# Two reorderings in a nine-stage fp32 transformer kernel: residual adds ahead of weight splits on VectorE, and table transposes behind the up block on TensorE

## The chip, the cores and the metric

The kernel runs on one core of one Trainium2 chip. The metric is the device time of one execution in microseconds (us), lower is better. PE is the matrix engine (TensorE), PEld its weight loads, ACT is ScalarE, DVE is VectorE, POOL is GpSimd, and SP is the engine that issues most of the DMAs (transfers between the chip's large memory and the on-chip buffer).

## The reference

Two transformer blocks run over 256 tokens of width 2048, all in fp32. What matters here are the three feed-forward networks, since the change lies in them:

```python
D_MODEL = 2048; SEQ = 256; D_FF = 4 * D_MODEL; D_FF_2 = 5632
def sqrelu_mlp(x, w_up, w_down):              # block 1, twice
    h = jax.nn.relu(x @ w_up)
    return (h * h) @ w_down
...
        x = layer_norm(DEEPNORM_ALPHA * x + h, ln_mix_g[i], ln_mix_b[i])
        x = layer_norm(DEEPNORM_ALPHA * x + sqrelu_mlp(x, w_up[i], w_down[i]), ...)
...
def _conv_ffn(h, w_up, conv_w, conv_b, w_down):   # block 2, once
    a = h @ w_up
    a = causal depthwise convolution of width 3 over the tokens (a) + conv_b
    gate, val = jnp.split(a, 2, axis=-1)
    return (jax.nn.silu(gate) * val) @ w_down
...
def _s5_group(...):   # block 2: 64 groups of 16 channels, 64 complex states each
    abar, bbar from lambda, dt, b;  s_t = abar * s_(t-1) + bbar * u_t;  y = Re(c s) + d u
```

Around them stand a pooling mixer, a dilated attention and a mixer of a state-space scan and a low-rank attention. The state-space scan is done four tokens at a step with small matrices ("tables") that follow from lambda, dt, b and c. Building these tables is independent of the tokens.

## The kernel before

All weights stream through four slots of 128 x 2048 values each (`raw`, 1 MB a slot). The matrix engine takes fp32 data as a sum of a high part and a low part, so each slot passes through four hands: SP loads `raw[s]`; ACT copies it rounded to `whi[s]` (`hi1`, L528); DVE subtracts the two to `wlo[s]` (`lo1`, L1028); PE does three matmuls for each product (L1807 to L1809 for up tiles, L1855 to L1857 for down tiles) and counts `chunk_used`. `hi1` of a slot waits until the previous use of the slot is over, and SP's next load of it waits for `lo1` (`lo_ready`). Four slots' worth of weights are a quad. The order on each engine is written out by hand, and semaphores (`then_inc`, `wait_ge`) tie the engines together.

The stages run one after the other: pooling, mlp0, attention, mlp1, the mixer, and ffn. In mlp0 and mlp1 the 8192 hidden features are done in 16 groups of 512. A turn of PE's loop does `up(g + 1)` (192 matmuls of 256 columns into PSUM banks 0 and 1) and `down(g)` (four chunks of 24 matmuls of 512 columns each). Chunk `s` of `down` makes 512 output columns for all tokens in two PSUM banks; it alternates between banks 4, 5 and banks 6, 7. DVE adds each finished chunk to `resid` (`add_down`, L1068) and thereby frees the banks through `down_free`. Chunk 2 may start only when the add of chunk 0 is done, chunk 3 only after that of chunk 1. ACT reads the up block (`activate`, L646 and L648: relu and square) and later rounds it for the next down (`split`). In ffn there are 11 groups, each with two up quads (gate and value), a convolution that ACT and DVE share (L986, L1654), and one down quad.

In mlp0 alone, 16 table jobs run beside the weights, one in each turn. POOL builds the operands `b_wide`, `c_wide` and `b_four` of a job from `compact`; `ssm_tables` on PE turns them and multiplies them (L1926 four transposes, L1931 the products, into banks 2 and 3); ACT's `table_out` copies the result out, stores it by DMA, and loads `compact` for the next job. The lines that close this ring are:

```python
# ACT, table_out(j), called after activate(g + 1)
act.wait_ge(job_turned, j + 1)
...
if not last:
    load_compact(j + 1)
# POOL, job j
pool.wait_ge(compact_landed, j * 16 + 16)
pool.wait_ge(tables_stored, j * 48 + 48)
...
pool.sem_inc(job_ready, 1)
# PE, ssm_tables(j)
pe.wait_ge(job_ready, j + 1)
pe.wait_ge(job_copied, j + 1)
```

Of the kernel before, what the change touches and what calls it, by code (L numbers as in the profile page):

```python
# [156 lines left out]
def build(nc, x_t, x_rows, gain_rows, weights, ssm_compact, ssm_skip, features, consts, dist_table, ssm_lam, positions, out):  # L157
    with ExitStack() as ctx:
# [130 lines left out]
        def wait_used(eng, q, s=SLOTS - 1):  # L289

            eng.wait_ge(chunk_used, q * SLOTS + (SLOTS + s + 1))
# [730 lines left out]
        def _(dve):  # L1022
            step = Steps(dve, dve_steps)

            def lo1(q, s, width=CW):

                dve.wait_ge(hi_ready, q * SLOTS + (s + 1))
                dve.tensor_tensor(wlo[:, s, 0:width], raw[:, s, 0:width], whi[:, s, 0:width].bitcast(F32),  # L1028
                                  ALU.subtract).then_inc(lo_ready, 1)
# [5 lines left out]
            def lo4_add(q, q_down, widths=(CW,) * 4):  # L1035

                for s in range(SLOTS):
                    lo1(q, s, widths[s])
                    add_down(q_down, s)

            def norm(name, gain, src, dst_hi, dst_lo, fill=False):
                k = NORM[name]
# [22 lines left out]
            def add_rows(nb, bank, sem_, n):  # L1065

                r = rows_of(resid, nb)
                return dve.tensor_tensor(r, r, ps[:, bank:bank + 2, :], ALU.add).then_inc(sem_, n)  # L1068
# [110 lines left out]
            def add_down(q, nb):  # L1179
                wait_used(dve, q, nb)  # L1180
                add_rows(nb, 4 + 2 * (nb % 2), down_free, 2)
# [200 lines left out]
            q, u = QUAD["pool_out"], UNITS["pool_out"]  # L1382
# [67 lines left out]
            q, u = QUAD["attn_out"], UNITS["attn_out"]  # L1450
# [26 lines left out]
            q, base = QUAD["mixer"], UNITS["mlp1"] + 120  # L1477
# [169 lines left out]
            def conv_rest(g, half_):  # L1647

                dve.wait_ge(conv_start, g * 2 + (half_ + 1))
                for lag, tap in ((1, 1), (2, 0)):  # L1650
                    for nt in range(4):
                        i = g * 4 + (half_ * (FF2 // P) + nt)
                        o = conv[:, 4 * half_ + nt, lag:T]
                        ins = dve.scalar_tensor_tensor(out=o, in0=block_ps(half_)[:, nt, 0:T - lag],  # L1654
                                                       scalar=fcol("ffn_conv_w_2", i + tap * (2 * FF2 // P)), in1=o,
                                                       op0=ALU.mult, op1=ALU.add)
                        if lag == 1:
                            step(ins)
                    if lag == 1:
                        step.settle()  # L1660
                ins.then_inc(conv_done, 1)
                dve.wait_ge(conv_done, g * 2 + (half_ + 1))
                dve.sem_inc(block_free, 1)

            def group(g, q, adds):

                conv_rest(g, 0)
                lo1(q, 0)
                dve.wait_ge(sig_ready, g + 1)
                if not (isinstance(g, int) and g == 0):  # L1670
                    dve.wait_ge(hidden_lo, g + h0)
                step(dve.tensor_tensor(hid[:], conv[:, 0:4, :], gate_sig[:], ALU.mult))
                for s in range(1, SLOTS):
                    lo1(q, s)
                conv_rest(g, 1)
                for s in range(SLOTS):
                    lo1(q + 1, s)
                    if adds:
                        add_down(q, s)
                    if s == 0:  # L1680
                        step.settle()
                        dve.tensor_tensor(hid[:], hid[:], conv[:, 4:8, :], ALU.mult).then_inc(hidden_ready, 1)
                dve.wait_ge(hidden_hi, g + (h0 + 1))
                dve.tensor_tensor(hid_lo[:], hid[:], hid_hi[:].bitcast(F32), ALU.subtract).then_inc(hidden_lo, 1)
# [15 lines left out]
            q, base = q0 + 3 * n - 1, UNITS["ffn"] + 8 * (n - 1)  # L1700
# [96 lines left out]
        def _(pe):  # L1797
# [137 lines left out]
            def mlp(name, tables=False):  # L1935
                q0, b0, h0, n = QUAD[name], BLOCK[name], HIDDEN[name], FF // HID

                def up(g):
                    quad_block(g * 2 + (q0 - 1), 0, g + (b0 + 2))
                block_first("mix" + name[-1], q0, b0 + 2)  # L1940
                if tables:
                    pe.wait_ge(table_landed, 48)
                with pe.Fori(0, n - 1) as g:
                    if tables:
                        ssm_tables(g)
                    up(g + 1)
                    down(g * 2 + (q0 + 2), g * 8 + UNITS[name], g + (h0 + 1))
                if tables:
                    ssm_tables(n - 1)
                down_last(q0 + 2 * n - 1, UNITS[name] + 8 * (n - 1), h0 + n, last_hi, last_lo)  # L1950
                if tables:
                    pe.wait_ge(job_copied, JOBS + 1)
                    pe.wait_ge(lags_copied, JOBS + 1)
# [13 lines left out]
            q, u = QUAD["pool_out"], UNITS["pool_out"]  # L1967
# [109 lines left out]
            q, u = QUAD["attn_out"], UNITS["attn_out"]  # L2077
# [355 lines left out]
```

## Time and profile before

| | |
|---|---|
| three runs | 3532.62 us median (3529.07 to 3534.78) |
| profiled execution, its own time | 3528.66 us |
| its span in the profile | 3526.8 us |
| PE busy | 3314.5 us, 94% of the span |
| DVE busy | 1950.6 us, 55% |
| ACT busy | 1461.2 us, 41% |
| POOL busy | 304.4 us, 9% |
| mean busy share of the DMA engines | about half, 174 GB/s |

The span runs from the first to the last instruction of the profiled execution; its own time is 1.9 us longer. PE's busy share is close to full, but the ends of matmuls are modelled, so PE shows as busy for a fraction of a microsecond after its last matmul has streamed. What counts as lost is therefore read from the starts of its instructions and from the waits. The clock that was granted to PE over the whole span is 0.976 of full speed.

### The profile page before, as it was taken

The numbers are of one execution on the slowest core, as the hardware profiler recorded it, in microseconds if no ns is written. First come the engines' busy times: TensorE is split into PE (matmuls) and PEld (weight loads), VectorE is DVE, ScalarE is ACT, GpSimd is POOL, SyncE is SP. The second block draws the span as 40 slices with busy tenths as digits, with TensorE's granted clock in tenths as the row PEclk, the third lists the DMA queues.
The fourth block names the chain that finished last, engine by engine and source line by source line (L and its number), as shares of the span: only waits on it lengthen the run. The fifth ranks groups of instructions, "written<-read, shape, count | busy, mean of one in ns | idle before, by whom it ended". The sixth has DMA issues, their size and how long they took to land.

```text
span 3526.8 us, 54501 instructions
## 1 busy us (share of the span) xinstructions
PE 3314.5 (94%) x22368; PEld 3029.7 (86%) x22368; DVE 1950.6 (55%) x1709; ACT 1461.2 (41%) x1281; POOL 304.4 (9%) x474
## 2 busy tenths in 40 slices
PE   6899999999999999989999999989789999999998
PEld 6778888788878999978988888869677899999897
DVE  7755444444455444546555555577445666655656
ACT  4334343434344434334443434434553444444442
POOL 1301312321330000000000000005000000000000
PEclk9999999999999999999999999999899999999999
DMA  6445555555554444445555555525223555555552
GB/s 255 146 165 202 184 186 177 184 184 186 178 183 156 180 168 158 168 156 203 189 186 184 190 182 187 189 96 219 107 94 132 191 183 186 186 183 189 180 190 95
DMA packets 117687, 613.40 MB, mean 174 GB/s; under 512 B 14480, under 2 KB 45264, under 8 KB 47184
## 3 DMA queue, kind: packets, MB, share of 16 engines
q1 hardware_dynamic: 94640, 594.79, 47.5%
q10 hardware_dynamic: 22944, 17.10, 1.5%
q8 instruction: 82, 1.34, 0.1%
q14 instruction: 21, 0.17, 0.0%
HBM read 599.26 MB, written 12.58 MB: 173 GB/s over the span
## 4 chain that ended last, share of the span: by engine, by line
PE 75%; DVE 6%; POOL 5%; ACT 4%; issue 4%; DMA 3%; ACTq 1%; POOLq 0%; SPq 0%; DVEq 0%
PE ps L1807 17%; PE ps L1809 16%; PE ps L1808 16%; PE ps L1855 7%; PE ps L1856 7%; PE ps L1857 7%; DMA compact<-ssm_compact 2%; POOL b_wide L1770 1%; DMA raw<-weights 1%; POOL b_four L1773 1%; POOL job_tmp L1766 1%; DVE wlo L1028 1%; POOL c_wide L1770 1%; ACT whi L528 1%; DVE conv L1654 1%
## 5 line engine op out<-in xcount | busy, mean ns | idle before, releaser
L1028 DVE TENSOR_TENSOR wlo<-raw,whi 128x2048 fp32r<-128x2048 f32 (+2 forms) x572 | 1254.7, 2199 | 1388.3 <-ACT whi L528 1382.3
L528 ACT ACTIVATE whi<-raw 128x2048 fp32r<-128x2048 f32 (+2 forms) x572 | 1044.0, 1830 | 1690.5 <-PE ps L1809 1007.4
L1807 PE MATMUL ps<-x_pair,whi 128*128 128x256 f32 x5104 | 1438.0, 282 | 56.4 <-DVE wlo L1028 34.2
L1809 PE MATMUL ps<-x_pair,wlo 128*128 128x256 f32 x5104 | 1430.8, 280 | 0.0
L1808 PE MATMUL ps<-x_pair,whi 128*128 128x256 f32 x5104 | 1430.7, 280 | 0.0
L1807 PEld LDWEIGHTS ps<-x_pair,whi 128*128 128x128 f32 x5104 | 963.2, 189 | 61.7 <-issue 52.1
L1808 PEld LDWEIGHTS ps<-x_pair,whi 128*128 128x128 f32 x5104 | 963.0, 189 | 1.3
L1809 PEld LDWEIGHTS ps<-x_pair,wlo 128*128 128x128 f32 x5104 | 963.4, 189 | 0.0
L1855 PE MATMUL ps<-whi,hid_hi 128*128 128x512 f32 x1312 | 529.7, 404 | 37.4 <-DVE resid L1068 30.6
L1857 PE MATMUL ps<-whi,hid_lo 128*128 128x512 f32 x1312 | 524.5, 400 | 0.0
L1856 PE MATMUL ps<-wlo,hid_hi 128*128 128x512 f32 x1312 | 524.3, 400 | 0.0
L1855 PEld LDWEIGHTS ps<-whi,hid_hi 128*128 128x128 f32 x1312 | 250.1, 191 | 112.9 <-DVE resid L1068 48.9
L1857 PEld LDWEIGHTS ps<-whi,hid_lo 128*128 128x128 f32 x1312 | 250.1, 191 | 61.6
L1856 PEld LDWEIGHTS ps<-wlo,hid_hi 128*128 128x128 f32 x1312 | 250.6, 191 | 57.0
L1068 DVE TENSOR_TENSOR resid<-resid,ps 128x1024 f32<-128x1024 f32 x171 | 207.4, 1213 | 0.0
L385 POOL TENSOR_TENSOR scan_room<-state,hop 128x64 f32<-128x64 f32 (+3 forms) x20 | 10.0, 500 | 1363.0 <-ACT state L862 1361.6
L1654 DVE SCALAR_TENSOR_TENSOR conv<-ps,feat,conv 128x255 f32<-128x255 f32 (+1 forms) x176 | 72.6, 475 | 2.7
L1781 POOL TENSOR_TENSOR inner_out<-inner_out,lag_out 128x256 f32<-128x256 f32 x16 | 11.8, 737 | 575.5 <-ACT lag_out L622 575.5
L1770 POOL TENSOR_TENSOR b_wide<-job_tmp 64x128 f32<-64x128 f32 x64 | 54.5, 852 | 4.9
L1773 POOL TENSOR_TENSOR b_four<-job_tmp 64x128 f32<-64x128 f32 x64 | 50.7, 792 | 0.0
L1855 PE MATMUL ps<-whi,x_pair 128*128 128x512 f32 x128 | 50.6, 396 | 0.0
L1856 PE MATMUL ps<-wlo,x_pair 128*128 128x512 f32 x128 | 50.6, 396 | 0.0
(341 smaller groups left out, 2421.9 us busy)
## 6 DMA issues: line engine op xcount, KB each, us to landing
raw<-weights SPq DMA_DIRECT2D x539, 1024.0 KB, 4.8
read_tab<-read_tables SPq DMA_DIRECT2D x2, 3072.0 KB, 12.4
raw<-weights SPq DMA_DIRECT2D x8, 640.0 KB, 8.0
drive_tables<-drive_out ACTq DMA_DIRECT2D x16, 256.0 KB, 6.0
read_tables<-c_wide ACTq DMA_DIRECT2D x32, 128.0 KB, 5.9
drive_tab<-drive_tables SPq DMA_DIRECT2D x4, 1024.0 KB, 6.8
x_in<-x_t SPq DMA_DIRECT2D x4, 512.0 KB, 6.9
resid<-x_rows ACTq DMA_DIRECT2D x1, 2048.0 KB, 14.0
```

The costliest lines, as they stand in the source:

```text
L528: act.activation(whi[:, s, 0:width], raw[:, s, 0:width], ACT.Copy).then_inc(hi_ready, 1)
L1028: dve.tensor_tensor(wlo[:, s, 0:width], raw[:, s, 0:width], whi[:, s, 0:width].bitcast(F32), ALU.subtract).then_inc(lo_ready, 1)
L1068: return dve.tensor_tensor(r, r, ps[:, bank:bank + 2, :], ALU.add).then_inc(sem_, n)
L1654: ins = dve.scalar_tensor_tensor(out=o, in0=block_ps(half_)[:, nt, 0:T - lag], scalar=fcol("ffn_conv_w_2", i + tap * (2 * FF2 // P)), in1= ...
L1770: step(pool.tensor_tensor(wide[rows, e, :, :, 16 * g:16 * g + 16], a[rows], b[rows], ALU.add))
L1773: step(pool.tensor_tensor(b_four[rows, e, :, :, 16 * g:16 * g + 16], a[rows, :, STEP - 1:STEP, :].to_broadcast(same), b[rows, :, STEP - 1: ...
L1807: pe.matmul(o, w_hi, x_hi, start=first, stop=False)
L1808: pe.matmul(o, w_hi, x_lo, start=False, stop=False)
L1809: return pe.matmul(o, w_lo, x_hi, start=False, stop=last)
L1855: pe.matmul(o, xh[:, k, t], whi[:, s, c], start=first and j == 0, stop=False)
L1856: pe.matmul(o, xh[:, k, t], wlo[:, s, c], start=False, stop=False)
L1857: ins = pe.matmul(o, xl[:, k, t], whi[:, s, c], start=False, stop=last and j == 3)
```

## The change

Two orders are changed; no instruction of arithmetic is added or taken away.

On DVE, in the loops of mlp0, mlp1 and ffn, the residual add of slot `s` now stands in front of the weight split of the same slot. On PE, in mlp0's loop, the job's transposes and products now stand behind the up block instead of in front of it. The job of the last turn, behind the loop, stays where it was.

```diff
             def lo4_add(q, q_down, widths=(CW,) * 4):
                 for s in range(SLOTS):
+                    add_down(q_down, s)
                     lo1(q, s, widths[s])
-                    add_down(q_down, s)
...
                 conv_rest(g, 1)
                 for s in range(SLOTS):
-                    lo1(q + 1, s)
                     if adds:
                         add_down(q, s)
+                    lo1(q + 1, s)
                     if s == 0:
                         step.settle()
                         dve.tensor_tensor(hid[:], hid[:], conv[:, 4:8, :], ALU.mult).then_inc(hidden_ready, 1)
...
                 with pe.Fori(0, n - 1) as g:
+                    up(g + 1)
                     if tables:
                         ssm_tables(g)
-                    up(g + 1)
                     down(g * 2 + (q0 + 2), g * 8 + UNITS[name], g + (h0 + 1))
                 if tables:
                     ssm_tables(n - 1)
```

In the program of DVE, in the loop of mlp0, the rows from the fourth split of the down quad on read as follows before. L1028 is a split (`lo1`), L1068 a residual add.

```order
205 L1028 TENSOR_TENSOR wlo<-raw,whi 128x2048
206 L1027 ISA
207 L1028 TENSOR_TENSOR wlo<-raw,whi 128x2048
208 L291 REGISTER_ALU
209 L1068 TENSOR_TENSOR resid<-resid,ps 128x2x512
210 L1027 REGISTER_ALU
211 L1028 TENSOR_TENSOR wlo<-raw,whi 128x2048
212 L291 REGISTER_ALU
213 L1068 TENSOR_TENSOR resid<-resid,ps 128x2x512
```

The same place in the changed kernel:

```order
205 L1028 TENSOR_TENSOR wlo<-raw,whi 128x2048
206 L291 REGISTER_ALU
207 L1068 TENSOR_TENSOR resid<-resid,ps 128x2x512
208 L1027 ISA
209 L1028 TENSOR_TENSOR wlo<-raw,whi 128x2048
210 L291 REGISTER_ALU
211 L1068 TENSOR_TENSOR resid<-resid,ps 128x2x512
212 L1027 REGISTER_ALU
213 L1028 TENSOR_TENSOR wlo<-raw,whi 128x2048
```

Each add has moved ahead of one split; the split of a slot and the add that waits for the same chunk have changed places, four times a turn.

In the program of PE, at the head of mlp0's loop (L1943 is the loop's entry, L1926 and L1931 are the table job, L1807 to L1809 the up block), before:

```order
1538 L1943 UNCONDITIONAL_BRANCH
1539 L1943 ISA
1540 L1926 MATMUL ps<-const,b_wide 128x128 x4
1541 L1931 MATMUL ps<-c_wide,b_four 128x128 x4
1542 L1834 REGISTER_ALU
1543 L1804 ISA
1544 L1807 MATMUL ps<-x_pair,whi 128x256
```

and in the changed kernel, at the end of the up block and the start of the down block (L1855 to L1857):

```order
1735 L1809 MATMUL ps<-x_pair,wlo 128x256
1736 L1926 MATMUL ps<-const,b_wide 128x128 x4
1737 L1931 MATMUL ps<-c_wide,b_four 128x128 x4
1738 L1804 ISA
1739 L1900 ISA
1740 L1855 MATMUL ps<-whi,hid_hi 128x512
1741 L1856 MATMUL ps<-wlo,hid_hi 128x512
```

The eight instructions of the job have moved behind the 192 matmuls of the up block and now stand directly ahead of the down block.

## Rows read from the trace of the kernel before

**Rows 1.** The page: the span and the number of instructions.

```profile
span 3526.8 us, 54501 instructions
```

**Rows 2.** The page's chain that ended last, shares of the span by engine.

```profile
PE 75%; DVE 6%; POOL 5%; ACT 4%; issue 4%; DMA 3%; ACTq 1%; POOLq 0%; SPq 0%; DVEq 0%
```

**Rows 3.** Busy time in the stretches of the mlp0, mlp1 and ffn loops.

```profile
core 0: us, PE busy (x) PEld busy (x) DVE busy (x) ACT busy (x) POOL busy (x), PEclk, DMA share, GB/s
288.00:1050.00 762.00, 715.77 (x4495) 635.92 (x4495) 373.02 (x200) 302.00 (x245) 206.94 (x315) 0.98 0.54 184
1638.00:2318.00 680.00, 678.80 (x4320) 608.23 (x4320) 369.01 (x199) 275.06 (x168) 0.00 (x0) 1.00 0.52 186
2780.00:3486.00 706.00, 704.57 (x5022) 657.34 (x5021) 439.64 (x373) 301.61 (x235) 0.00 (x0) 1.00 0.52 183
```

**Rows 4.** The relu of ACT, one a turn, in mlp0 and in mlp1.

```profile
L646 ACT ACTIVATE hid<-ps x15: 1003/1027/1032, 314.5 to 1024.6; 128x1024 f32<-128x1024 f32 x15
...
L646 ACT ACTIVATE hid<-ps x15: 1002/1004/1007, 1665.2 to 2297.4; 128x1024 f32<-128x1024 f32 x15
```

**Rows 5.** Waits in mlp0, 288 to 1050 us: total, times, longest.

```profile
PE ps L1855 <- DVE resid L1068: 29.3, 15, 2.3
PEld ps L1926 <- POOLq L1778: 21.7, 15, 2.4
PE ps L1926 <- POOLq L1778: 15.1, 14, 2.0
```

**Rows 6.** Timeline of ACT in one turn of mlp0: start, duration.

```profile
566.11 1.91 ACT L528 ACTIVATE whi<-raw 128x2048 fp32r<-128x2048 f32 x1 [3.74 <-PE ps L1809]
...
573.69 1.92 ACT L528 ACTIVATE whi<-raw 128x2048 fp32r<-128x2048 f32 x1 [1.94 <-issue]
```

**Rows 7.** Timeline of DVE in the same turn.

```profile
575.63 2.29 DVE L1028 TENSOR_TENSOR wlo<-raw,whi 128x2048 fp32r<-128x2048 f32 x1 [5.29 <-ACT whi L528]
577.84 1.21 DVE L1068 TENSOR_TENSOR resid<-resid,ps 128x1024 f32<-128x1024 f32 x1
```

**Rows 8.** Timeline of PE in the same turn.

```profile
576.88 0.40 PE L1857 MATMUL ps<-whi,hid_lo 128*128 128x512 f32 x1
579.11 0.50 PE L1855 MATMUL ps<-whi,hid_hi 128*128 128x512 f32 x1 [1.84 <-DVE resid L1068]
...
591.73 0.40 PE L1857 MATMUL ps<-whi,hid_lo 128*128 128x512 f32 x1
592.69 0.66 PE L1926 MATMUL ps<-const,b_wide 128*128 128x128 f32 x4 [0.56 <-POOLq L1778]
...
593.99 0.36 PE L1807 MATMUL ps<-x_pair,whi 128*128 128x256 f32 x1
```

**Rows 9.** Timeline of POOL in the same turn: first and last instruction of the job.

```profile
578.38 0.41 POOL L1765 TENSOR_TENSOR job_tmp<-compact,z_pow 128x128 f32<-128x128 f32 x1 [5.82 <-DMA compact<-ssm_compact]
...
591.47 1.12 POOL L1770 TENSOR_TENSOR c_wide<-job_tmp 64x160 f32<-64x160 f32 x2
```

**Rows 10.** Two of 13 stretches behind the add wait; columns as in Rows 3.

```profile
580.50:583.50 3.00, 3.00 (x9) 2.36 (x8) 2.48 (x2) 0.00 (x0) 2.76 (x4) 0.51 0.75 270
630.00:634.00 4.00, 3.84 (x17) 3.12 (x18) 3.46 (x3) 0.01 (x1) 3.85 (x4) 1.00 0.91 283
```

**Rows 11.** Waits in mlp1, 1650 to 2290 us, and ffn, 2800 to 3480 us.

```profile
PEld ps L1855 <- DVE resid L1068: 6.6, 28, 0.3
...
PEld ps L1855 <- DVE resid L1068: 5.8, 10, 0.6
```

**Rows 12.** Timeline of PE in ffn, from chunk 1 to chunk 2 of a down quad.

```profile
2998.28 0.40 PE L1857 MATMUL ps<-whi,hid_lo 128*128 128x512 f32 x1
...
2999.18 0.39 PE L1856 MATMUL ps<-wlo,hid_hi 128*128 128x512 f32 x1
```

**Rows 13.** The end of ffn: timelines of DVE and PE.

```profile
3490.76 1.21 DVE L1068 TENSOR_TENSOR resid<-resid,ps 128x1024 f32<-128x1024 f32 x1
...
3493.16 0.80 PE L1855 MATMUL ps<-whi,hid_hi 128*128 128x512 f32 x1 [6.65 <-DVE hid_lo L1684]
```

## The prediction

> **What bounds the kernel now.** I read the view of the stages first, then the chain, the waits of PE in each loop, and last the timelines of one turn. The span is 3526.8 us [rows 1]. The chain that ended last is PE for 75% of it, and POOL stands on it with 5%, or some 176 us [rows 2], although of the three feed-forward loops it works in one alone [rows 3]. So in mlp0 work runs through POOL while PE could have more to do. The stages show where: in mlp1 and ffn PE is busy for 99.8% of the stretch and its granted clock is 1.00, the upper of its two levels, 2.4 GHz; in mlp0 it is busy for 715.77 of 762 us and the clock is 0.98 [rows 3]. The reader is to see that mlp0 and mlp1 do the same matrix work, and that one is slower.
>
> By how much, the relu of ACT tells, which comes once a turn. In mlp0 15 of them start between 314.5 and 1024.6 us, 14 turns of 50.72 us; in mlp1 between 1665.2 and 2297.4 us, 14 turns of 45.16 us [rows 4]. The table job of mlp0 takes PE from 592.69 to 593.99 us, 1.30 us [rows 8]. So 50.72 - 45.16 - 1.30 = 4.26 us of each turn are lost to something else.
>
> Three things make it up. PE waits for a residual add in every turn, 29.3 us over 15 waits, 1.95 us each; and it waits for POOL's job in nearly every turn, 15.1 us over 14, 1.08 us each [rows 5]. The clock is the third: in the 3 us behind the add wait of one turn it is 0.51, so at the lower level of 1.2 GHz, and in another turn it is 1.00 [rows 10]. Of the 13 turns that I looked at in this way, 9 show 0.51 to 0.69. Over the loop 0.98 means 2% of 762 us, 15 us, or 1.0 us a turn [rows 3]. 1.95 + 1.08 + 1.0 = 4.0 us; 0.2 us remain, and the weight loads do wait somewhat longer than the matmuls (21.7 against 15.1 us in the case of POOL [rows 5]).
>
> **Why these waits are there.** The add: chunk 1 of the down block has its last matmul at 576.88 us, and chunk 2 starts at 579.11 us, when the add of chunk 0 is through [rows 8]. That add starts at 577.84 us, since it stands behind the split, which starts at 575.63 us [rows 7], which waits for ACT's rounding at 573.69 us [rows 6]. Chunk 0 had been ready for long: up and down stream the same number of columns, so each takes half of 45.16 us, 22.6 us, and a chunk 5.65 us. The down block started near 566.0 us, as ACT's rounding of the last up slot shows [rows 6], so chunk 0 was done near 571.7 us. ACT's 2 us of rounding, DVE's 2.2 us of splitting and ACT's table work all stand between it and an add that needs none of them.
>
> The job: the ring is up block, relu and copies on ACT, load of `compact`, POOL's 20 operations (578.38 to 592.59 us [rows 9]), transposes, next up block. From the end of the up block to the start of the transposes it takes 592.69 - 566.1 = 26.6 us, and the ring closes with 1.30 us of table work and 22.6 us of up block: 50.5 us, the measured turn. **So mlp0 turns at the pace of this ring, and not of PE's own work.** Taking away the add wait alone would only lengthen the wait for POOL. Both edits are needed together.
>
> **The change, part by part.**
>
> *Transposes behind the up block.* The job of turn g is now wanted a full up block later. The ring no longer runs through POOL within a turn: a job has the whole turn, 46.4 us, for its 26.6, a cover of 19.8 us. On ACT the copy of the tables stands behind a rounding and the two operations of `activate`, 4 us past the end of the up block; the transposes and products now take the first 1.3 us of that time, so the copy isn't late by them. Its five DMA issues, and whatever SP has queued, keep their places: no queue is moved past. The down block starts 1.3 us later and the up block 1.3 us earlier; both sums stay. If the cover were gone, each us of it would cost 1 us a turn.
>
> *Adds ahead of the splits.* The split of a slot waits for ACT's rounding, which waits for the same chunk. The add waits for that chunk alone, so it fits in the 1.9 us in which ACT rounds. In mlp0 the add of chunk 0 ends near 7.1 + 1.3 us after the up block's end, and chunk 2 wants it 12.6 us after. The add wait goes, and with it, I take it, the lower clock, since mlp1, whose turns have no wait of PE of that length, holds 1.00 [rows 3].
>
> New turn of mlp0: 45.16 + 1.30 = 46.46 us, less 0.1 us of add wait that mlp1's own turn still holds (below). 50.72 - 46.4 = 4.3 us. It applies to the 14 turns from the first to the last relu that I counted: 60 us. Ahead of them nothing changes, since the first up block of the loop waits for the relu's banks either way. Behind the last relu little changes: the last job still stands behind the last down block of the loop, its ring of 26.6 us is as long as before, and PE is now at its door after 1.3 + 22.6 = 23.9 us. It waits 2.7 us there instead of 1 to 2, but starts the last table work at the same moment. Unknown is the length of that job: POOL's operations take 0.4 us or, beside a split on DVE, some 2 us more. I bound this at 2 us to either side.
>
> *The same adds in mlp1 and ffn.* In ffn, chunk 1's last matmul starts at 2998.28 us, and the second of chunk 2 at 2999.18 us [rows 12]. Two steps of 5.65 / 24 = 0.235 us would be 0.47; 0.43 us are lost, in each of ten turns: 4.3 us. The bound above is the wait of the weight loads, 5.8 us; below it is 0. In mlp1 the loads wait 6.6 us in 28 waits, two a turn, of 0.24 us [rows 11]. In ffn 0.15 of 0.58 us of each such wait cost the matmuls nothing; the same off 0.24 leaves 0.09 us, 28 times, 2.5 us. I take 2 us, between 0 and 6.6.
>
> *The end.* After the last ffn turn PE waits 6.65 us for `hid_lo`, which stands on DVE behind the add of chunk 3, 1.21 us at 3490.76 us [rows 13]. The add now runs while ACT rounds the last slot, and PE starts 1.2 us sooner. The clock is low there, so it may be 0 to 3 us.
>
> Sum: 60 + 4.3 + 2 + 1.2 = 67.5 us. The profiled execution took 3528.66 us, 1.9 us more than its span, so 3461 us; the median of the three runs is 4 us above that one and would give 3465 us. **I say 3463 us.**
>
> **Rivals.**
>
> *The lower clock stays.* All 15 us of it: 3463 + 15 = 3478 us. For it: in 4 of 13 turns the same wait of 2 us left the clock alone [rows 10], so the wait isn't the whole cause, and two blocks are now separated by small matmuls of the job. Against it: mlp1 has no such time at all. The Trainium skill, "TensorE: Matmul & The Clock Gate", section "A second HAM failure mode: psum-queue depth-cycling", says that frequent short idles between groups of matmuls can make the clock swing between its levels. By that rule, the clock stays low as long as any short idles are left, and the time would be this rival's; in mlp1, with idles of 0.2 us twice a turn, the trace doesn't agree.
>
> *Only one of the two waits goes.* If the ring through POOL still closed a turn (say, because the job's copies on ACT come so late that the cover of 20 us is used up), mlp0 would stay at 50.7 us and only 4.3 + 2 + 1.2 us would be gained: 3521 us against 3528.66, about 3523 on my middle. Against it speak the 19.8 us.
>
> *Slower: the splits come late.* Where ACT's rounding is already there when DVE arrives, the add ahead delays the split by 1.21 us, and with it `lo_ready`, SP's next load of the slot and PE's next use. There are some 160 such adds; if each were on the path, 160 x 1.21 = 194 us would be added, 3463 + 194 = 3657 us at the worst. It decides from the point where a split has less than 1.2 us of slack. The split of slot 0 ends at 577.92 us and PE wants it at 593.99 us, 16 us later [rows 7, 8], some 12 us in the new turn. It would need a third of the splits on the path to end slower than now.
>
> **How the numbers follow.** The forecast has 0.79; the clock that stays 0.11; one wait only 0.07, half of it by more than 0.2%; slower 0.03. This kernel's measurement can tell about 0.2%, 7 us, from no change. So faster is 0.79 + 0.11 + 0.035 = 0.935, same 0.035, slower 0.03. The range: downwards the bounds of mlp1, ffn, the end and the last job give 3461 - 8 = 3453 us; upwards it takes in the clock that stays, 3480 us.
>
> **What would show it.** In the changed profile the relus of mlp0 should stand 46.4 us apart, 14 turns in 650 us, with PE's clock at 0.99 or 1.00 in the loop. No wait of PE for the residual add in mlp0, mlp1 or ffn, and one for POOL instead of 14, of 2 to 4 us, ahead of the last job. PE's wait for `hid_lo` at the end near 5.4 us. POOL's share of the chain should fall from 5% to under 1%. The prediction is wrong if the relus are still 50 us apart (the ring is closed elsewhere), if ACT's table copy waits for the transposes by more than 0.5 us, if `whi` waits for weight loads, which now come at 9% more MB a second, or if the clock in the loop is still 0.98.

## The result: 1.85% faster, as forecast in sum

| | before | after |
|---|---|---|
| median, executions interleaved on one chip | 3530.85 us (4: 3524.75 to 3534.78) | 3464.62 us (4: 3463.76 to 3466.21) |
| profiled execution, its own time | 3528.66 us | 3466.21 us |
| its span | 3526.8 us | 3464.4 us |

The ratio is 0.9815, with a 95% interval of 0.9802 to 0.9827. The forecast was 3463 us, with a range of 3453 to 3480 us.

The page of the changed kernel, its parts 1 (busy time of POOL, last entry) and 4 (the chain that ended last), answers to [rows 1, 2]:

```profile
span 3464.4 us, 54486 instructions
...
PE 3293.8 (95%) x22368; PEld 3029.7 (87%) x22368; DVE 1970.0 (57%) x1709; ACT 1461.4 (42%) x1281; POOL 321.3 (9%) x474
...
PE 89%; DVE 5%; ACT 3%; DMA 2%; issue 1%; POOL 0%; SPq 0%; ACTq 0%; DVEq 0%; POOLq 0%
```

POOL has left the chain, where it held 5%, and PE has gone from 75% to 89%. POOL itself is busy for 321.3 us, 17 us more than before: its work has got slower, and hardly anybody waits for it. That is worth remembering for the first experiment.

The relus of the changed kernel, mlp0 and mlp1, answer to [rows 4]:

```profile
L646 ACT ACTIVATE hid<-ps x15: 1009/1029/1032, 314.5 to 963.6; 128x1024 f32<-128x1024 f32 x15
...
L646 ACT ACTIVATE hid<-ps x15: 1003/1005/1006, 1608.8 to 2239.0; 128x1024 f32<-128x1024 f32 x15
```

A turn of mlp0 takes (963.6 - 314.5) / 14 = 46.36 us instead of 50.72, a turn of mlp1 45.01 instead of 45.16. Over 14 turns that is 61.0 us in mlp0 and 2.0 us in mlp1.

The windows of the changed kernel in the same three loops (columns as in [rows 3]):

```profile
300.00:960.00 660.00, 660.00 (x4297) 599.16 (x4296) 357.52 (x185) 282.57 (x226) 207.80 (x294) 1.00 0.59 199
1581.00:2250.00 669.00, 667.29 (x4280) 602.50 (x4281) 368.52 (x196) 273.26 (x167) 0.00 (x0) 1.00 0.53 187
2730.00:3425.00 695.00, 695.00 (x4964) 650.71 (x4963) 435.51 (x371) 296.97 (x231) 0.00 (x0) 1.00 0.52 184
```

PE is busy through the whole of mlp0's loop, at a clock of 1.00. Its waits from 270 to 1000 us, which answer to [rows 5]:

```profile
PE ps L1926 <- POOLq L1778: 5.4, 1, 5.4
PE ps L1807 <- ACT hid L646: 3.1, 1, 3.1
```

Both kinds of wait of [rows 5] are gone from the turns. One wait for POOL is left, ahead of the last job, and the wait of the first turn for the relu has grown from 1.7 to 3.1 us, since no table job stands ahead of it any more. And at the end of ffn:

```profile
PE ps L1855 <- DVE hid_lo L1684: 5.5, 1, 5.5
```

It was 6.65 us [rows 13].

**Where the gain was given back.** The roundings L998 of ffn start from 2830.7 to 3488.4 us before and from 2774.2 to 3427.8 us after, 657.7 and 653.6 us: 4.1 us. With the 1.1 us at the end the gains come to 61.0 + 2.0 + 4.1 + 1.1 = 68.2 us; the span is shorter by 62.4. Some 4.5 us of the difference lie between the last relu of mlp0 and the first transpose of `resid` on PE (L1870) behind mlp0: 1024.6 to 1073.1 us before, 48.5 us; 963.6 to 1016.6 us after, 53.0 us. They have two parts. From the end of the last up block to the last table job it is 26.7 us before (1022.63 to 1049.30 us) and 29.0 after (961.63 to 990.66 us), so 2.4 us are a job that is ready later. From the table job to L1870 it is 23.8 us before and 25.9 after, 2.1 us for the same work: that is the clock, which is low when PE comes back from a wait of 5.4 us.

The rest, 1.3 us, lies where nothing was changed or is the sum of small differences: from the last relu of mlp1 to the first rounding of ffn it takes 535.2 us instead of 533.3, attention is 0.1 us longer, and from the last rounding of ffn to the end of the span the gain is 1.8 us, 0.7 us more than the shorter wait.

The first turn lost time too, though not in this sum. From the first relu of mlp0 to the second, before and after:

```profile
L646 ACT ACTIVATE hid<-ps x2: 1003/1004/1005, 288.6 to 314.5; 128x1024 f32<-128x1024 f32 x2
L646 ACT ACTIVATE hid<-ps x2: 1005/1007/1009, 287.1 to 314.5; 128x1024 f32<-128x1024 f32 x2
```

It takes 27.4 us instead of 25.9; in the execution that was profiled mlp0 began 1.5 us sooner, which hides it. The windows at both ends show the clock. Before:

```profile
270.00:300.00 30.00, 28.26 (x240) 28.06 (x240) 19.22 (x10) 13.47 (x9) 0.00 (x0) 1.00 0.62 235
...
1020.00:1075.00 55.00, 50.89 (x242) 41.06 (x240) 33.91 (x35) 21.97 (x22) 14.54 (x22) 1.00 0.41 136
```

and after:

```profile
960.00:1015.00 55.00, 49.60 (x223) 40.68 (x223) 30.09 (x30) 21.07 (x22) 16.89 (x22) 0.94 0.38 126
270.00:300.00 30.00, 26.91 (x215) 26.69 (x214) 20.23 (x11) 12.50 (x8) 0.00 (x0) 0.94 0.56 215
```

The clock of 1.00 in the loop has its price at both its ends: 2.1 us behind the last job and 1.5 us in the first turn, after waits that are now longer (5.4 us for the last job, 3.1 us for the relu). 6% of a window would be more than that, because part of the low clock falls into the wait itself, where it costs nothing.

### The profile page after: what moved, and what is told of

Same layout as the page of the kernel before. It is cut to its first block, busy times and chain, and to the rows that moved or that the text cites. A ratio compares the mean times of both kernels' runs of the same rounds, so it can differ in the third digit from the quotient of the medians.

```text
span 3464.4 us, 54486 instructions
## 1 busy us (share of the span) xinstructions
PE 3293.8 (95%) x22368; PEld 3029.7 (87%) x22368; DVE 1970.0 (57%) x1709; ACT 1461.4 (42%) x1281; POOL 321.3 (9%) x474
## 4 chain that ended last, share of the span: by engine, by line
PE 89%; DVE 5%; ACT 3%; DMA 2%; issue 1%; POOL 0%; SPq 0%; ACTq 0%; DVEq 0%; POOLq 0%
PE ps L1807 17%; PE ps L1809 17%; PE ps L1808 17%; PE ps L1855 11%; PE ps L1856 11%; PE ps L1857 11%; DMA raw<-weights 1%; DVE wlo L1028 1%; ACT whi L528 1%; ACT y_mix L874 1%; PE ps L1931 0%; PE ps L2119 0%; PE ps L1846 0%; PE ps L2041 0%; DVE row_stats L1079 0%
## 5 line engine op out<-in xcount | busy, mean ns | idle before, releaser
L1028 DVE TENSOR_TENSOR wlo<-raw,whi 128x2048 fp32r<-128x2048 f32 (+2 forms) x572 | 1259.4, 2207 | 1099.0 <-ACT whi L528 1095.3
L1807 PE MATMUL ps<-x_pair,whi 128*128 128x256 f32 x5104 | 1440.8, 282 | 56.8 <-DVE wlo L1028 32.6
L1809 PE MATMUL ps<-x_pair,wlo 128*128 128x256 f32 x5104 | 1432.9, 281 | 0.0
L1807 PEld LDWEIGHTS ps<-x_pair,whi 128*128 128x128 f32 x5104 | 966.3, 189 | 62.5 <-issue 52.9
L1809 PEld LDWEIGHTS ps<-x_pair,wlo 128*128 128x128 f32 x5104 | 966.9, 189 | 0.0
L1855 PE MATMUL ps<-whi,hid_hi 128*128 128x512 f32 x1312 | 520.0, 396 | 5.5 <-DVE hid_lo L1684 5.5
L1857 PE MATMUL ps<-whi,hid_lo 128*128 128x512 f32 x1312 | 518.5, 395 | 0.0
L1068 DVE TENSOR_TENSOR resid<-resid,ps 128x1024 f32<-128x1024 f32 x171 | 208.7, 1221 | 198.7 <-PE ps L1857 195.7
L1855 PEld LDWEIGHTS ps<-whi,hid_hi 128*128 128x128 f32 x1312 | 246.5, 188 | 64.5 <-DVE hid_lo L1684 6.0
L1857 PEld LDWEIGHTS ps<-whi,hid_lo 128*128 128x128 f32 x1312 | 246.3, 188 | 60.4
L385 POOL TENSOR_TENSOR scan_room<-state,hop 128x64 f32<-128x64 f32 (+3 forms) x20 | 10.1, 503 | 1362.9 <-ACT state L862 1361.5
L1773 POOL TENSOR_TENSOR b_four<-job_tmp 64x128 f32<-64x128 f32 x64 | 59.1, 924 | 0.0
L1770 POOL TENSOR_TENSOR c_wide<-job_tmp 64x160 f32<-64x160 f32 x64 | 51.8, 810 | 4.9
L758 ACT ACTIVATE qkv_t<-ps 128x768 f32<-128x768 f32 x24 | 19.5, 811 | 74.6 <-PE ps L1809 74.6
L1855 PE MATMUL ps<-whi,x_pair 128*128 128x512 f32 x128 | 50.4, 394 | 0.0
## 6 DMA issues: line engine op xcount, KB each, us to landing
resid<-x_rows ACTq DMA_DIRECT2D x1, 2048.0 KB, 14.2
```

What stands on the lines that cost most here:

```text
L1770: step(pool.tensor_tensor(wide[rows, e, :, :, 16 * g:16 * g + 16], a[rows], b[rows], ALU.add))
L1773: step(pool.tensor_tensor(b_four[rows, e, :, :, 16 * g:16 * g + 16], a[rows, :, STEP - 1:STEP, :].to_broadcast(same), b[rows, :, STEP - 1: ...
L1807: pe.matmul(o, w_hi, x_hi, start=first, stop=False)
L1809: return pe.matmul(o, w_lo, x_hi, start=False, stop=last)
L1855: pe.matmul(o, xh[:, k, t], whi[:, s, c], start=first and j == 0, stop=False)
L1857: ins = pe.matmul(o, xl[:, k, t], whi[:, s, c], start=False, stop=last and j == 3)
```

## The experiments

All of them were timed against the kernel before, on one chip with it. "The changed kernel" is 3464.62 us.

### 1 and 2. Each edit alone

`e1_adds_only` takes the table edit back:

```diff
                 with pe.Fori(0, n - 1) as g:
-                    up(g + 1)
                     if tables:
                         ssm_tables(g)
+                    up(g + 1)
```

> The kernel before with the adds moved ahead of the splits in all three loops, and the table job of mlp0 left in front of the up block. Theory 1 (ring): mlp0 turns at the pace of the ring through GpSimd (50.5 of 50.72 us in the profile of before), so taking the add wait away only lengthens TensorE's wait for the job. Expected: relus of mlp0 still 50.2 to 51.2 us apart, no wait for the residual add, waits for POOL of some 3 us a turn instead of 1.1; gains only in mlp1, ffn and at the end, 6 to 9 us, so 3522 to 3525 us against the 3530.9 us of before. Rival (sum): each wait is worth its own time, 29 us of add waits and a share of the lower clock in mlp0, so 3480 to 3494 us and turns of 48 to 48.8 us.

**Measured: 3585.65 us (3581.26 to 3586.62), ratio 1.0149 [1.0132, 1.0165].** Neither was right: the adds alone make the kernel 55 us slower. The relus of mlp0 and the waits of PE there:

```profile
L646 ACT ACTIVATE hid<-ps x15: 1003/1029/1035, 313.8 to 1085.5; 128x1024 f32<-128x1024 f32 x15
...
PE ps L1926 <- POOLq L1778: 96.9, 14, 7.3
```

A turn takes 55.12 us, and PE waits 6.9 us in each for POOL. The add wait is gone indeed, but the ring through POOL has become longer than it was. POOL's timeline of one turn shows how:

```profile
600.69 0.42 POOL L1765 TENSOR_TENSOR job_tmp<-compact,z_pow 128x128 f32<-128x128 f32 x1 [5.69 <-DMA compact<-ssm_compact]
...
601.98 2.50 POOL L1773 TENSOR_TENSOR b_four<-job_tmp 64x128 f32<-64x128 f32 x1
604.56 0.46 POOL L1770 TENSOR_TENSOR b_wide<-job_tmp 64x128 f32<-64x128 f32 x1
...
605.61 0.47 POOL L1765 TENSOR_TENSOR job_tmp<-compact,c_pow 128x160 f32<-128x160 f32 x1 [0.16 <-POOL b_four L1773]
...
612.99 2.52 POOL L1766 TENSOR_TENSOR job_tmp<-compact,c_pow 128x160 f32<-128x160 f32 x1
615.59 1.97 POOL L1770 TENSOR_TENSOR c_wide<-job_tmp 64x160 f32<-64x160 f32 x2
```

and DVE's, beside it:

```profile
601.69 2.48 DVE L1028 TENSOR_TENSOR wlo<-raw,whi 128x2048 fp32r<-128x2048 f32 x1 [0.27 <-ACT whi L528]
605.40 1.22 DVE L1068 TENSOR_TENSOR resid<-resid,ps 128x1024 f32<-128x1024 f32 x1 [1.24 <-PE ps L1857]
...
612.88 2.31 DVE L1028 TENSOR_TENSOR wlo<-raw,whi 128x2048 fp32r<-128x2048 f32 x1 [0.65 <-ACT whi L528]
615.11 1.49 DVE L1189 TENSOR_TENSOR hid_lo<-hid,hid_hi 128x1024 fp32r<-128x1024 f32 x1
```

A POOL instruction of 0.46 us that meets a split takes 2.5 us: it ends just behind the split and not before. The add at 605.40 us, which reads one of its inputs from PSUM, holds nothing up: the POOL instruction at 605.61 us takes 0.47 us. The last pair of the job (615.59 us, 1.97 us instead of 1.12) meets the subtraction of `hid_lo`, which also reads both inputs from SBUF. The job lasts from 600.69 to 617.56 us, 16.9 us instead of 14.2 [rows 9], since without the add wait chunks 2 and 3 end sooner and one more split lies beside the job. From the end of the up block (588.5 us) to the transposes (617.66 us) it is 29.1 us where it was 26.6. That is 2.5 us of the 4.4 by which the turn grew. The rest is in the windows of the wait and of what follows it:

```profile
300.00:1080.00 780.00, 683.14 (x4274) 616.72 (x4273) 352.95 (x186) 282.45 (x226) 232.54 (x294) 0.93 0.49 168
...
613.80:617.60 3.80, 0.00 (x0) 0.00 (x0) 2.79 (x2) 0.00 (x0) 3.61 (x3) 0.51 0.47 140
617.70:620.60 2.90, 2.90 (x14) 2.90 (x15) 0.00 (x0) 0.00 (x0) 0.00 (x0) 0.50 0.62 260
620.60:624.00 3.40, 3.40 (x30) 3.40 (x30) 0.00 (x0) 0.00 (x0) 0.00 (x0) 0.99 0.00 0
```

PE waits from 610.9 to 617.66 us, and comes back at the lower level, 1.2 GHz, for some 3 us, in which the job and the start of the up block run. The up block is part of the ring, so the slower clock delays the next job as well.

`e2_tables_only` keeps the table edit and puts the adds back behind the splits, in ffn in the same way as here:

```diff
                 for s in range(SLOTS):
-                    add_down(q_down, s)
                     lo1(q, s, widths[s])
+                    add_down(q_down, s)
```

> The kernel before with the table job moved behind the up block, and the adds left behind the splits. Theory 1 (ring): the turn of mlp0 becomes TensorE's own work, 46.36 us as in the changed kernel, plus the add wait of 1.95 to 2.2 us, so 48.4 us with the clock at full, 49.4 us if the lower clock still follows the add wait. Gain 14 x 1.3 to 2.3 = 18 to 33 us: 3498 to 3513 us. With e1 this makes 24 to 42 us, less than the 66 us of both together. Rival (sum): e1 and e2 add up to 66 us. A second question is the clock: if it needs both waits of a turn, TensorE's clock in the loop is 1.00 here, if the add wait alone brings it down, it stays at 0.98.

**Measured: 3479.84 us (3476.07 to 3481.25), ratio 0.9855 [0.9839, 0.987].** Better than every expectation: the table edit alone gains 51 of the 66 us. Its waits in mlp0:

```profile
PE ps L1855 <- DVE resid L1068: 8.1, 15, 0.8
...
PE ps L1926 <- POOLq L1778: 1.9, 1, 1.9
```

The add wait is down from 1.95 us to 0.54 us a turn though nothing on DVE was moved. The down block starts 1.3 us later, behind the job, while ACT begins its table work and roundings as early as before; I put the smaller wait down to that; no run tests it. The turn is (974.9 - 315.0) / 14 = 47.14 us at a clock of 1.00. So waits of 0.5 us, every turn, leave the clock alone.

The edits alone give +55 and -51 us and together -66 us. The adds are worth -15 us beside the table edit and +55 us without it.

### 3. The length of the job and the clock, apart

Both kernels start from `e1_adds_only`. `e7_short_splits` makes the splits of the up weights in mlp0's loop 16 columns wide instead of 2048, so that POOL meets no long split on DVE. The low parts of those weights are not computed.

```diff
-                    lo4_add(g * 2 + (q0 + 3), g * 2 + (q0 + 2))
+                    lo4_add(g * 2 + (q0 + 3), g * 2 + (q0 + 2), (16,) * 4 if name == "mlp0" else (CW,) * 4)
```

> The kernel of e1 in which the four splits of each up quad in mlp0's loop are done on 16 of the 2048 columns only; the low parts of the up weights are wrong there, and nothing else differs. In e1 POOL's job takes 16.9 us, with three or four operations of 2.2 to 2.5 us where a split of VectorE runs beside them, and 0.4 to 0.5 us otherwise. Theory: POOL's operation waits for the split beside it. Without the splits the job takes some 10.5 us, the ring is 6 us shorter, PE no longer waits for POOL more than 1 us, and the turn comes to 46.4 to 47.5 us: 3585 - 14 x 8 = 3465 to 3480 us. Rival: POOL's long operations have another cause (the weights' DMAs beside them) and the job stays near 17 us, the turn near 55 us.

**Measured: 3465.31 us (3463.05 to 3466.3), ratio 0.9821 [0.9806, 0.9836].** Every POOL instruction is short again. First and last of one job:

```profile
602.57 0.42 POOL L1765 TENSOR_TENSOR job_tmp<-compact,z_pow 128x128 f32<-128x128 f32 x1 [5.81 <-DMA compact<-ssm_compact]
...
611.55 1.13 POOL L1770 TENSOR_TENSOR c_wide<-job_tmp 64x160 f32<-64x160 f32 x2
```

The job takes 10.1 us, the turn (966.1 - 312.7) / 14 = 46.67 us, and of the waits for POOL 1.1 us are left in five places of the loop, and 6.4 us ahead of the last job. The weights still stream beside POOL's work, at 198 GB/s in the loop against 168 in the first experiment, so the rival that the transfers make POOL slow is out. The 120 us between this kernel and the first experiment hang on what DVE does while POOL works.

The Trainium skill, "SBUF — State Buffer", section "Who interferes with whom", says that VectorE and GpSimd share one pair of ports, held for a whole instruction, so that the one that comes second blocks until the first is done; by the page's section "Summary: rules for kernel authors" this holds for a VectorE instruction with two SBUF inputs against a GpSimd instruction that reads SBUF. The traces agree: 0.46 us becomes 2.5 us beside a split and stays 0.47 beside the add.

`e6_filled_wait` puts 24 matmuls of 512 columns, whose results nobody reads, on PE ahead of each table job in the loop:

```diff
                     if tables:
+                        pe.wait_ge(job_copied, g + 1)
+                        for i in range(24):
+                            pe.matmul(ps[:, 2, :], xhi[:, i % 16, 0:P], ..., start=True, stop=True)
                         ssm_tables(g)
```

> The kernel of e1 (adds moved, table job in front of the up block) with 24 extra matmuls of 512 columns, 5.65 us, put on TensorE in front of each table job of the loop, into a free PSUM bank; their results are not used. e1 turns in 55.12 us, and TensorE waits 7 us there for POOL's job. My theory of e1: of the 4.4 us a turn that it lost against the kernel before, some 2.6 are a longer job of POOL, and some 1.9 are the lower clock, which follows the 7 us wait and falls on the up block, which is part of the ring. With the wait filled, the clock should stay at 1.00, the turn should fall to 29.1 + 1.3 + 22.6 = 53.0 us, 14 x 2.1 = 30 us: 3550 to 3560 us, although TensorE does 85 us more work. Rival: the clock has no part in it, the turn stays at 55 us and the time at 3586 us.

**Measured: 3568.06 us (3561.76 to 3574.06), ratio 1.0117 [1.0101, 1.0132].** The windows and the relus of the loop:

```profile
300.00:1060.00 760.00, 740.42 (x4645) 660.10 (x4644) 355.61 (x185) 282.31 (x226) 232.01 (x294) 1.00 0.51 173
...
L646 ACT ACTIVATE hid<-ps x15: 1012/1027/1032, 315.0 to 1063.2; 128x1024 f32<-128x1024 f32 x15
```

PE does 24 matmuls more in each turn and the turn is shorter, 53.44 us instead of 55.12, at a clock of 1.00, while POOL's long instructions are as before (604.34 us, 2.52 us, in one job). So 1.7 of the 4.4 us were the clock. With the 2.5 us of the longer job that is 4.2 of 4.4 us. The kernel as a whole missed what was expected, 3550 to 3560 us: the turn was to be 53.0 us, and the median is 6 us above the profiled execution, 3561.76 us, which is the fastest of the four. By the medians the filling is worth 17.6 us, 1.3 us a turn.

### 4. The cover of the job

The prediction took a cover of 19.8 us as proof that POOL would leave the path. Three kernels use it up by issuing the load of `compact` later in ACT's turn. In the last two a turn loads the operands of its own job, so the load ahead of the loop goes as well; all else is as in the changed kernel.

```diff
                         inner_store(g)
+                        load_compact(g + 1)     # e9_late_load; taken out of table_out
...
+                    for s in range(SLOTS):      # in place of hi4 for the next down quad
+                        hi1(g * 2 + (q0 + 2), s)
+                        if tables and s == 0:   # e10_later_load: 0; e11_latest_load: 1
+                            load_compact(g)
```

> The changed kernel with ScalarE's load of the next job's compact operands issued behind the turn's second rounding instead of in front of its first, some 20 us later in the turn. In the changed kernel a job is ready 29.1 us after the end of the up block and is wanted after 46.4 us, so it has 17.3 us of cover. Theory (ring): 20 us use the cover up, the job comes 2 to 4 us too late in each turn, TensorE waits for POOL again and the turn comes to 48.5 to 51 us: 14 x 2.1 to 4.6 = 30 to 65 us, 3495 to 3530 us. Rival: what was won has nothing to do with the distance between the job and its use, and the time stays within 5 us of 3465 us.

> The changed kernel with the load of compact for the job of a turn issued still later: behind ACT's first rounding of the next down quad, that is after chunk 0 of the up block behind which the job's tables are wanted. In the run before, the load was issued 17.5 us later in the turn, POOL's job then ended near 589.8 us and the transposes started at 592.96 us, 3.2 us of cover left, at 46.36 us a turn. Here the load moves by one more slot, 5.1 us. If the cover is as worked out, the job ends 2 us behind the up block and PE waits about 1.5 to 2 us in each of 14 turns; the path that closes is load, job, transposes within one turn, so the wait is paid once a turn: turns of 48.0 to 48.5 us, and up to 1 us more where PE's clock falls after a wait of that length: 23 to 42 us in all, 3490 to 3509 us. Rival: the job gets shorter where fewer splits of DVE lie beside it (it is 14.6 us there, 10.1 with none): no wait, 3467 us.

> As the run before, but the load stands behind ACT's second rounding, one slot of 5.65 us later again. The job then ends 7 to 8 us behind the up block: turns of 53.5 to 54.5 us, with the lower clock after each wait up to 56, 14 x 7.2 to 9.5 us = 100 to 135 us above the changed kernel: 3565 to 3600 us. Rival (the ring isn't bound by the load's place): below 3500 us.

| load issued | median us | ratio | mlp0 turn us | wait for POOL us a turn |
|---|---|---|---|---|
| as in the changed kernel | 3464.62 | 0.9815 | 46.36 | 0 |
| 17.5 us later in the turn | 3467.2 (3463.76 to 3469.75) | 0.9819 [0.9804, 0.9834] | 46.36 | 0 |
| one slot later | 3491.14 (3486.61 to 3492.32) | 0.9882 [0.9862, 0.9902] | 48.38 | 1.4 |
| two slots later | 3593.61 (3589.53 to 3594.43) | 1.0171 [1.0151, 1.019] | 55.56 | 7.0 |

The first missed what the ring was to give there: nothing was lost. In the changed kernel a load is issued at 551.49 us, 7.24 us behind transposes at 544.25; in the late one at 571.34, 24.72 us behind transposes at 546.62. That is 17.5 us later, and the job was done in time nevertheless. POOL's last instruction starts at 588.66 us, and PE's next transposes at 592.96:

```profile
588.66 1.13 POOL L1769 TENSOR_TENSOR c_wide<-job_tmp 64x160 f32<-64x160 f32 x2
...
592.96 0.60 PE L1925 MATMUL ps<-const,b_wide 128*128 128x128 f32 x4
```

3.2 us were left. The next two kernels were forecast from that and came out so. One slot more costs 2.0 us a turn on the mean and 1.6 in the turns behind the first (from transposes at 559.87 us to transposes at 607.81 us it is 47.94 us, with a wait of 1.4 us), because the first turn waits 4.8 us. Two slots cost 9.2 us a turn, of which 7.0 are wait and the rest goes with the clock, which is 0.93 in that loop:

```profile
300.00:1080.00 780.00, 682.17 (x4223) 615.56 (x4222) 347.20 (x184) 281.69 (x224) 193.94 (x294) 0.93 0.47 166
...
PE ps L1929 <- POOLq L1781: 97.8, 14, 7.2
```

So the cover is real. In the changed kernel it is 590.60 - 572.85 = 17.75 us in one turn (from POOL's end to the transposes), where the prediction had 19.8: the job takes 16.1 us there (from 556.71 us) and not 14.2. The late load got 2.9 us more, since its job met two long instructions instead of three (14.6 us) and the load landed 1.4 us sooner; that is why 17.5 us could be spent with 3.2 left.

### 5. ffn

`e4_ffn_as_before` is the changed kernel with ffn's order put back (the second hunk of the diff reversed).

> The changed kernel with the order of ffn as before (split ahead of add there alone). Theory: 0.4 us in each of ten turns and 1 to 2 us at the end come back, 5 to 6 us: 3470 us, and TensorE's weight loads wait 5 to 6 us for the residual add in ffn again. Rival: the ffn part was worth nothing and the gain that stands there in the profile is another's: 3464 to 3466 us.

**Measured: 3472.86 us (3469.3 to 3474.97), ratio 0.983 [0.9816, 0.9843].** The roundings L998 span 657.8 us again, against 653.6, and the two waits are back:

```profile
PEld ps L1855 <- DVE resid L1068: 5.8, 10, 0.6
...
PE ps L1855 <- DVE hid_lo L1684: 6.7, 1, 6.7
```

The edit in ffn is worth 4.2 us in the turns and 1.2 us in the last wait; the medians differ by 8 us, and the intervals of the two ratios overlap, so that 5.4 us isn't contradicted, and isn't shown by the times either.

### 6. The last job and the first turn

`e3_last_job_mid` puts the last job between the two token halves of the last down block, 48 matmuls later, where POOL is done:

```diff
+            def down_last(q, u, hidden, hi, lo, between=None):
...
                 for tt in range(2):
+                    if tt and between is not None:
+                        between()
...
-                if tables:
-                    ssm_tables(n - 1)
```

> The changed kernel with the last table job of mlp0 moved from in front of the last down block to between its two token halves, 11.3 us later. In the changed kernel TensorE waits 5.4 us there for POOL, and a stretch at the lower clock follows (4.6 us of it behind the job, 2.2 us ahead), worth some 3.4 us. Theory: the wait and the clock's share go, 5.4 + 3 = 8 to 9 us: 3456 us (3454 to 3460). Rival: ScalarE, which copies the tables out before it takes the square root of the first rows, comes 6 us later to the norm behind mlp0 and gives 3 to 6 us of it back: 3460 to 3463 us.

**Measured: 3454.87 us (3453.59 to 3462.56), ratio 0.9787 [0.9771, 0.9802].** From the last relu (964.5 us) to L1870 (1009.8 us) it is now 45.3 us, not 53.0: the wait of 5.4 us is gone and so is the low clock behind it.

`e5_first_and_last` also peels the first turn and leaves job 0 in front of its up block, where PE waits for the relu in any case.

> The kernel of e3 (both orders changed, last table job between the two halves of the last down block) with mlp0's first turn written out ahead of the loop and its table job left in front of that turn's up block, where TensorE waits 3.1 us for ScalarE's relu anyway. Theory: the 1.3 us of the first job disappear into that wait, and the lower clock that followed it in the changed kernel (3.4 us, worth 1.7) may go too: 1.3 to 3 us less than e3's 3454.9 us, 3452 to 3454 us. Rival: the program grows by some 300 instructions and nothing is gained: 3455 us or more.

**Measured: 3462.13 us (3459.37 to 3465.87), ratio 0.981 [0.9796, 0.9823].** A miss against the kernel before it in this list, on which it was to improve; the intervals of the two ratios touch, so the trace has to say what happened. mlp0 did end sooner (L1870 at 1006.5 us instead of 1009.8, and 2.3 us sooner when counted from mlp0's first relu), and attention, which nobody had touched, took 9.0 us longer: from the first L1870 behind mlp0 to the first behind attention 537.9 us instead of 528.9. PE's timeline behind the start of a loop in attention:

```profile
1302.80 0.28 PE L1808 MATMUL ps<-x_pair,whi 128*128 128x256 f32 x1
1304.69 0.58 PE L1809 MATMUL ps<-x_pair,wlo 128*128 128x256 f32 x1 [1.61 <-issue]
```

PE halts for 1.9 us in the middle of a chain of equal matmuls, with nothing that the trace shows to wait for, after 11 matmuls behind the start of a loop; behind the start at 1182.16 us it halts after as many, for 2.6 us. In `e8_shifted` 72 increments of a semaphore that nobody reads are strewn into the peeled down block, where matmuls hide them; they shift the place of PE's later code.

```diff
                     ins = pe.matmul(o, xl[:, k, t], whi[:, s, c], start=False, stop=last and j == 3)
+                    if j < 3:
+                        for _ in range(pad):        # 3 in the peeled block, else 0
+                            pe.sem_inc(pad_count, 1)
```

> The kernel of e5 with 72 increments of an unused semaphore strewn between the matmuls of mlp0's first down block on TensorE, where a matmul takes 0.235 us and the increments should be hidden. They only shift what follows in TensorE's program. In e5 the attention stage took 537.8 us against 529.0 in e3: at two of the loop's starts TensorE stood still for 2.6 and 1.9 us in the middle of a product, some 12 matmuls behind the loop's first one, waiting for nothing that the profile shows, and a stretch at the lower clock followed. Theory: this is the delivery of the program's instructions, and it depends on where the loop lies. With the shift these two halts go, attention comes back to 529 to 530 us, and the total to 3452 to 3455 us. Rival: the halts have to do with the work (the turn ahead of the loop, the weights), and the time stays at 3462 us.

**Measured: 3448.93 us (3445.54 to 3452.09), ratio 0.9766 [0.9753, 0.978].** The halts are gone, and attention is back at 528.0 us (1006.9 to 1534.9). This is the fastest kernel of the study, 16 us below the changed one. Attention gives 9.9 of the 13.5 us between the two profiled executions; 4.2 us lie in the mixer behind mlp1 (529.9 us from the last relu to ffn's first rounding, instead of 534.1), and their cause is open. That the halts have to do with how instructions reach PE fits "issue" as the releaser and their going away with a shift; it is argued from one shift, and which limit is met there was not shown.

## Why the prediction was right, and where it wasn't

**What bounds mlp0: right.** The ring through POOL closed the turn. The turn fell to 46.36 us (46.4 said), the clock of the loop rose to 1.00, and POOL's share of the chain went from 5% to 0. With POOL's job short and the table job where it was, `e7_short_splits` turns in 46.67 us. The cover experiments show the same ring coming back once the load is late by more than 17.5 us.

**The terms.** mlp0 61.0 us (60 said), mlp1 2.0 (2), ffn 4.1 (4.3), the end 1.1 (1.2). The total came closer than its parts allow, and that is partly luck: the terms said add up to 67.5 us, 5 more than the profiled pair differs by (62.4 us), while the medians differ by 66.2.

**"Starts the last table work at the same moment": wrong.** From the end of the last up block to the last tables it is 29.0 us (961.63 to 990.66) and not the 26.7 of before, because three of POOL's instructions meet a split and not two. PE waits 5.4 us there (2.7 said, with 2 us of bound) and comes back at the low clock: 2.4 + 2.1 us. "Ahead of them nothing changes" was wrong by 1.5 us: the table job no longer fills part of the first turn's wait for the relu, the wait grows to 3.1 us, and the low clock follows. So 3.6 of the 15 us of clock went back. I had counted the clock as a cost of the loop alone and not looked for a wait outside it that would grow.

**"Taking away the add wait alone would only lengthen the wait for POOL": wrong in its size.** The wait for POOL did grow, from 15 to 97 us, but by far more than the add wait it replaced, and the kernel became 55 us slower. The prediction had the row for it (POOL's instructions take 2 us more beside a split) and used it as an error bar of the last job, not as a term of the ring. Here the sum came out right because both edits were made and the longer job lies in the cover.

**"Both edits are needed together": wrong.** The table edit alone gives 51 of the 66 us, and the add wait shrinks with it from 1.95 to 0.54 us a turn. Only the adds need the other edit.

**The lower clock.** The add wait was given as the cause. The runs show more than one wait that the low clock follows, and where it follows and where not. It followed each of the longest waits looked at: 3.1 us for the relu, 5.4 us for the last job, 6.9 and 7.0 us for POOL in the turns of the first experiment and of the latest load (0.93 in both loops). It did not follow 0.54 us for the adds (clock 1.00), nor 1.4 us for POOL: the loop of `e10_later_load` shows 0.99, but all of it comes from the first turn with its wait of 4.8 us (0.93 from 300 to 348 us), and the next 13 turns show 1.00 each. In between, the length does not decide. In the kernel before, the add waits were 1.8 to 2.3 us long; 9 of 13 had the low clock behind them, and the longest had not. Five waits for POOL in that loop were as long, 1.80 to 1.97 us, and the clock behind each was 1.00. One of them, and the window right behind it:

```profile
643.48 0.65 PE L1926 MATMUL ps<-const,b_wide 128*128 128x128 f32 x4 [1.86 <-POOLq L1778]
643.40:646.40 3.00, 2.92 (x25) 2.92 (x26) 2.80 (x2) 1.11 (x2) 0.00 (x0) 1.00 0.58 218
```

What decides for a wait of 2 us was not tested. That the wait is the cause is shown for the longest alone, where filling it brought back 1.00. The prediction's rival "the lower clock stays" didn't come.

**Slower, because splits come late:** no sign of it. In ffn and mlp1 the turns got shorter.

## What to carry to other kernels

Two waits on one engine in one turn are not two terms of a sum: take the longer ring away first, and look at what a shorter wait moves on the other engines. An edit that is worth 15 us beside another can cost 55 us alone.

Where GpSimd works on a path, lay its instructions against VectorE's two-input work from SBUF before counting them: 0.46 us each is the price only of those that meet none.

When a loop is cured of its waits, read the first and the last turn by themselves. What they wait for stays or grows (here from 1.7 to 3.1 us and from 1.8 to 5.4 us), and the clock they lose is taken from the loop's gain. The mean clock of a loop can come from its first turn alone.

## What the hardware showed beyond that

A GpSimd instruction of 0.46 us took 2.5 us beside a VectorE subtraction of 2.3 us with both inputs in SBUF, and 0.47 us beside an addition with one input in PSUM.

In the wait of 6.8 us for POOL the granted clock went to 0.51 before the wait was over, and stayed at 0.50 for about 3 us of matmuls after it. Filling the wait with matmuls that nobody needs kept 1.00, and made the turn 1.7 us shorter. Waits of 1.8 to 2.0 us had the low clock behind them in some turns and not in others.

PE halted for 1.9 and 2.6 us in the midst of straight code behind the start of a loop. With 72 semaphore increments put in front the halts were gone, and the kernel went from 3462.13 to 3448.93 us, 9.9 us of it in the stage with the halts.
